# Eleven gate tiles moved out of the first attention into the delta net's levels, with the scan products of both directions on one bank

## The reference

```
mod = silu(c) @ w_ada + b_ada           # shift, scale, gate for both norms
h  = rmsnorm(x, norm_mix) * (1 + sc1) + sh1          # likewise hc from ctx
p  = h @ w_in                            # q,k,v | conv q,k,v | z | a,b | gates
qkv_d = silu(short_conv(qkv_d, conv_w)); q_d, k_d = l2norm(...)
g_attn, g_dn = split(sigmoid(gates + b_gate))
o_attn = windowed_attention(q, k, v, k_ctx, v_ctx, sink)
o_dn = gated_delta(q_d, k_d, v_d) forwards + backwards, context chunks first
     # per chunk: t_inv = inverse of unit lower triangular (A + I)
     # W = t_inv @ (k*beta*exp(G)); U = t_inv @ (v*beta)
     # v_new = U - W S;  o = q S + attn v_new;  S = S*g + k_tail v_new
x += gt1 * ((g_attn * (o_attn @ w_br_attn) + g_dn * (o_dn @ w_br_dn)) @ w_out)
```

## Time and profile before

| what | value |
|---|---|
| median of 3 runs | 1781.78 us (1777.49 to 1782.66) |
| profiled execution | 1772.43 us, its span 1770.6 us |
| PE busy | 1700.2 us, 96% |
| DVE, ACT, POOL busy | 1308.8, 1057.5, 161.3 us |
| bytes moved | 283.31 MB, mean 160 GB/s |
| projection's matmuls (L497) | 44.9 us to 256.4 us of the span |
| levels | about 261.5 us to 379.4 us of the span |

### The profile page before, as it was taken

How to read it: one execution, slowest core, us unless ns; L and a number is a source line. 1 busy time by engine, 2 the same in 40 slices (tenths; PEclk the granted TensorE clock), 3 DMA queues, 4 the chain that set the end, 5 groups by cost and what they waited for, 6 DMA issues and landing times.

```text
span 1770.6 us, 34144 instructions
## 1 busy us (share of the span) xinstructions
PE 1700.2 (96%) x11488; PEld 1513.5 (85%) x11488; DVE 1308.8 (74%) x2648; ACT 1057.5 (60%) x2182; POOL 161.3 (9%) x136
## 2 busy tenths in 40 slices
PE   7999997899999999999999999999899999999998
PEld 1877776689999978888899999999799899999997
DVE  3787677767989799667766666666776768878887
ACT  2545454445665699666555555555557666666666
POOL 0000003411548200000000000000010000010000
PEclk9999999999999999999999999999999999999999
DMA  8534441215455511455555555555364544555553
GB/s 303 186 99 140 156 154 60 84 47 199 161 178 178 166 37 48 166 191 196 193 185 185 189 189 184 186 188 189 119 209 142 176 141 133 177 184 185 187 181 129
DMA packets 77272, 283.31 MB, mean 160 GB/s; under 512 B 8576, under 2 KB 8576, under 8 KB 76928
## 3 DMA queue, kind: packets, MB, share of 16 engines
q1 hardware_dynamic: 77184, 282.16, 47.6%
HBM read 281.08 MB, written 1.05 MB: 159 GB/s over the span
## 4 chain that ended last, share of the span: by engine, by line
PE 80%; DVE 12%; ACT 4%; issue 2%; POOL 1%; DMA 1%; PEld 0%; PEldq 0%; ACTq 0%; POOLq 0%; DVEq 0%; SPq 0%
PE banks L921 20%; PE banks L909 17%; PE banks L1000 10%; PE banks L497 8%; PE banks L1156 7%; PE banks L1180 3%; PE banks L851 2%; DVE split L2444 2%; DVE arena L2440 2%; PE banks L465 1%; PE banks L1014 1%; PE banks L1116 1%; PE banks L821 1%; PE banks L541 1%; POOL split L2967 1%
## 5 line engine op out<-in xcount | busy, mean ns | idle before, releaser
L1529 ACT ACTIVATE split<-arena 128x512 fp32r<-128x512 f32 x492 | 308.9, 629 | 134.9 <-PE banks L909 76.8
L909 PEld LDWEIGHTS banks<-split 128*128 128x128 f32 x2880 | 355.4, 192 | 10.5 <-DVE split L2370 3.1
L921 PE MATMUL banks<-split 128*128 128x512 f32 x1536 | 361.9, 390 | 1.0 <-issue 1.0
L909 PE MATMUL banks<-split 128*128 128x256 f32 x2880 | 358.7, 283 | 3.2 <-DVE split L2370 2.3
L2462 DVE TENSOR_TENSOR split<-arena,split 128x512 fp32r<-128x512 f32 x396 | 270.6, 690 | 105.3 <-ACT split L1529 99.5
L921 PEld LDWEIGHTS banks<-split 128*128 128x128 f32 x1536 | 283.8, 188 | 57.3 <-issue 1.4
L1507 ACT ACTIVATE split<-arena 128x512 fp32r<-128x512 f32 x312 | 194.5, 627 | 112.3 <-PE banks L1156 52.9
L1000 PE MATMUL banks<-split 128*128 128x256 f32 x1728 | 216.8, 287 | 4.3 <-DVE split L2540 3.9
L1000 PEld LDWEIGHTS banks<-split 128*128 128x128 f32 x1728 | 211.9, 194 | 7.2 <-issue 6.0
L2517 DVE TENSOR_TENSOR split<-arena,split 128x512 fp32r<-128x512 f32 x180 | 123.7, 698 | 65.6 <-ACT split L1507 64.1
L497 PEld LDWEIGHTS banks<-split 128*128 128x128 f32 (+1 forms) x936 | 134.0, 194 | 28.5 <-issue 13.8
(11 more groups left out here) (421 smaller groups left out, 2311.5 us busy)
## 6 DMA issues: line engine op xcount, KB each, us to landing
arena<-wstream SPq DMA_DIRECT2D x525, 512.0 KB, 3.3
arena<-x_t SPq DMA_DIRECT2D x1, 2048.0 KB, 12.2
arena<-matsa SPq DMA_DIRECT2D x1, 1234.0 KB, 6.3
out_t<-arena SPq DMA_DIRECT2D x4, 256.0 KB, 2.0
arena<-mats SPq DMA_DIRECT2D x1, 576.0 KB, 8.1
arena<-crow SPq DMA_DIRECT2D x1, 512.0 KB, 7.1
arena<-rows SPq DMA_DIRECT2D x1, 512.0 KB, 3.9
arena<-mats SPq DMA_DIRECT2D x1, 449.0 KB, 4.3
```

Of the source, the lines that this page charges most:

```text
L909: mm = pe.matmul(ps[:, 4 + b, 0:S], w_parts[:, c, (2 * m + half) % 4, P * k:P * k + P], h_parts[:, e, 4 * half + k, :], start=(half == 0 a ...
L921: mm = pe.matmul(ps[:, 2 * tt + half, :], g_parts[:, e, j % 2, P * tt:P * tt + P], w_parts[:, c, (2 * m + half) % 4, :], start=(first and ...
L1529: act.activation(w_parts[:, 0, (2 * m + half) % 4, :], ring[:, peer_slot(m), 512 * half:512 * half + 512], ACT.Copy).then_inc(sem["w_hi"], 1)
```

## The change

1. The order of the stream is a list, `ORDER`. Behind tile t it puts the tails of `TAILS_BEHIND[t]`: one for POOL behind each of t = 10 to 17, three for DVE behind each of 25 to 28, and the other twelve between tiles 29 and 38. SP frees a tail's slot on `tail_sum` (POOL's) or `tail_done` (DVE's).
2. Twelve tails are now a multiplication on POOL and a sum on ACT (`sum_tail`): eight in `in_out(10)` to `in_out(17)`, one in level 3 of each block. DVE has twelve in the attention (three a group) and eight in the levels. `crow` is loaded and its SiLU taken early.
3. The attention keeps tiles 23, 24 and 25 (one in each of groups 0 to 2) and 26 (behind group 3); tile 27 stands where 38 stood.
4. Tiles 28 to 38 go into the levels as quarters of six matmuls on bank 7 (`fill_quarter`): one ahead of the level updates (`fill_before`) and one behind them (`fill_behind`). ACT rounds and moves out (`fill_hi`, `fill_out`), DVE subtracts one half in each level (`in_lo`).
5. Scan products of both directions share bank 6, one direction a level; `apply_inverse` writes banks 2d + 1 and 2d, so that the next block's products wait for `wu_ready` in place of `w_moved`. `z_turned` is folded into `y_done`. Half of the gates' sigmoid moves behind the levels.

```diff
+TAILS_BEHIND = {**{t: [("pool", t - 10)] for t in range(10, 18)}, **{t: [("dve", 3 * (t - 25) + q) for q in range(3)] for t in range(25, 29)}, ...
+ORDER = [x for t in range(39) for x in [("in", t)] + TAILS_BEHIND.get(t, [])]
             def load_freed_by_splits(lo, hi):
                 for n in range(lo, hi):
+                    kind, q = ORDER[n - RING - N_WIN]
+                    if kind == "in":
+                        sp.wait_ge(sem["in_lo"], 2 * q + 2)
+                    elif kind == "pool":
+                        sp.wait_ge(sem["tail_sum"], q + 1)
                     else:
+                        sp.wait_ge(sem["tail_done"], q + 1)
                     sp.dma_start(tile_at(n), wstream[n]).then_inc(loaded[n % RING], 16)
+            def fill_quarter(t, q):
+                if q == 0:
+                    pe.wait_ge(sem["proj_free"], 4 + t)
+                    ...
+                if q % 2 == 0:
+                    pe.wait_ge(sem["in_lo"], 2 * t + q // 2 + 1)
+                for k in (2 * q, 2 * q + 1):
+                    for c, e in PASSES:
+                        mm = pe.matmul(ps[:, 7, 0:S], ...)
+            def fill_before(step):
+                j, q = (step // 2, 1) if step % 2 else (step // 2 - 1, 3)
+                if 0 <= j < N_FILL:
+                    fill_quarter(FIRST_FILL + j, q)
+            def fill_behind(step):
+                if step // 2 < N_FILL:
+                    fill_quarter(FIRST_FILL + step // 2, 2 * (step % 2))
...
                     for d in range(2):
                         level_products(n, l, d)
+                    step = 6 * n + l - 1
...
+                    if n == 1 and l < 3:
+                        state_write(0, l - 1)
+                    if n >= 2 and l < 3:
+                        state_read(n - 1, l - 1)
+                    if n >= 2 and 3 <= l < 5:
+                        state_write(n - 1, l - 3)
+                    if n == 3 and l >= 5:
+                        out_write(2, l - 5)
...
+                    fill_before(step)
                     for d in range(2):
                         level_update(n, l, d)
...
+                    fill_behind(step)
 ACT, in in_out(t):
                 if 8 <= t < 20:
                     conv_silu(t - 8)
+                if 10 <= t < 18:
+                    sum_tail(t - 10)
+            def sum_tail(q):
+                tile = tile_at(AT["pool", q])
+                act.wait_ge(sem["tail_mult"], q + 1)
+                act.activation(tile, tile, ACT.Copy, accum_out=modT[:, ...]).then_inc(sem["tail_sum"], 1)
 ACT, in each level:
+                    if step % 2 == 0 and 0 < step <= 2 * N_FILL:
+                        fill_out(FIRST_FILL + step // 2 - 1)
+                    if 2 <= step < 2 * N_FILL - 2:
+                        fill_hi(step + 2)
...
+                    if l == 3:
+                        sum_tail(8 + n)
                     for d in range(2):
                         if n < 3 and l == 3:
                             decays(n + 1, d)
 DVE, in group g of the attention:
+                if g < 3:
+                    both_lo(25 + g)
+                for q in range(3):
+                    mod_tail(3 * g + q)
 DVE, in each level:
+                    i = 6 * n + l
+                    if 4 <= i < 2 * N_FILL:
+                        in_lo(FIRST_FILL + i // 2, i % 2)
+                    if l in (4, 6):
+                        mod_tail(12 + 2 * n + l // 6)
 POOL:
+            def mod_tail(q):
+                n = AT["pool", q]
+                pool.wait_ge(loaded[n % RING], 16 * (n // RING + 1))
+                pool.tensor_tensor(tile_at(n), tile_at(n), crow, ALU.mult).then_inc(sem["tail_mult"], 1)
+            pool.wait_ge(sem["conv_used"], 1)
+            for q in range(8):
+                mod_tail(q)
```

More of the change, by code:

```diff
@@ L1391, in _ @@
             tok_move(1)
-            in_out(38)
+            in_out(27)
             tok_move(2)
@@ L2179, in _ @@
             link(dve.tensor_copy(masks[:, :, 0:P], blocks))
-            tails = iter(range(EARLY_TAILS, 32))
-            for q in range(2):
-                mod_tail(next(tails))
+            both_lo(28)
             link(dve.tensor_tensor(gain3[:, 0, :], col("final_norm"), col("final_norm"), ALU.mult))
```

277 lines of the change are left out of this document (141 added, 136 removed).

## The result

Median of four executions 1814.63 us (1811.33 to 1817.49) against 1781.43 before: ratio 1.019, 95% interval 1.0164 to 1.0215. The forecast was 1800 with a range from 1776 to 1814: the sign was right, the size too small (18.5 us forecast, 33.2 measured). The profiled execution took 1816.22 us (span 1814.6), the one before 1772.43 (span 1770.6). These two are 43.8 us apart, the medians 33.2, since the profiled one of before was 9 us faster than its median. The stages are compared in the two traces; why other executions of before are slower is not seen in them.

What follows compares the result with a forecast made beforehand. PE was taken to bound the kernel (busy 96% of the span), with waits for DVE in the levels. Terms 19 - 2 - 24 + 0 + 25 + 0.5 = +18.5 us, put on the median 1781.8: 1800 us, range 1776 to 1814.

Steps and rivals of the forecast that it cites:

- The ring loop: Convolutions: each ACT step from tile 11 waits for a whole DMA, 8.0 us a tile against 5.49; +19 us.
- up to 0.9 us a tile: Convolutions: extra DVE time from POOL's multiplications beside its taps, hidden in the 8.0 us period, otherwise costing 3 us.
- Up to the first group: Ahead of the attention's first group: two tails leave from in front of DVE's logits(1), for which PE waits; -2 us.
- The attention: From the first group to the phase end: PE loses 34.3 us of work, less new waits and slow clock; -24 us.
- (c): Attention: PE's idle times bring slow-clock stretches as in tile 23; 3 us allowed.
- (a): Attention, group 1: the fourth product of scores(2) waits for DVE's logits(2); PE waits 3.8 us.
- (b): Attention, group 3: ACT's exponentials, logarithm and table loads delay first transposes 1.6 us and first weigh 3.8 us.
- Prologue: Prologue: two tails leave (2.4 us), both_lo(28) and both_lo(29) come (2.4); 0 us.
- The levels: Levels: quarters come on top where PE is full and fill only some idle time; +25 us, bounds 6 and 34.
- R1: Rival, convolutions: the ring's loop does not bind, they cost 0 to 3 us; total 1782; chance 0.15.
- R2: Rival, levels: quarters fit into PE's waits for DVE, costing 6 us in place of 25; down to 1772; chance 0.14.
- R3: Rival: idle times in convolutions and attention bring long slow clock, ten times, 15 us; 1815; chance 0.14 with another rival.

Runs made afterwards that it cites:

- e1: Changed kernel with ACT summing each POOL tail of the convolutions one tile earlier: ratio 1.0155 to the kernel before, tile 20 at 151.6.
- e4: e1 with POOL's eight convolution multiplications done on 8 of 1024 columns: span 1793.7, tile 20 at 139.8; no ratio taken.
- e6: Changed kernel with ACT's logarithm in group 1, DVE's squares behind logits(2), group 2's tails behind its output scaling: ratio 1.0137 to the kernel before, attention 67.0 us.
- e8: e6 with tile 26 in group 3 and tile 27 from the prologue behind it: ratio 1.014 to the kernel before.
- e12: e8 plus level 3's decays first and all tails on DVE, placed where it was seen idle: ratio 0.9975 to the kernel before, median 1773.95 us.
- e10_no_quarters: Changed kernel without the quarters' matmuls, ACT's and DVE's work for them kept: levels 141.7 us against 149.4; no ratio taken.
- e3_one_of_six: Changed kernel with one matmul of six in each quarter, ACT's and DVE's work kept: levels 144.85 us against 149.4; no ratio taken.

## Why the prediction was wrong, point by point

- **The ring loop (+19): right in mechanism.** Period 8.0 to 8.4 for a forecast 8.0, and e1 shows that it bound; from tile 13 to tile 19 the roundings fell behind by 15.1 us, as forecast. The term was +23.1, because POOL's price was wrong: "up to 0.9 us a tile" was read from a DVE tail that met only part of a POOL instruction. A whole meeting costs 2.0 to 2.2 us. Two meetings came ahead of the loop (1.8 and 2.1 us, from 87 to 92), where nothing hides them, and that is the 4 us. Without the loop POOL costs 11.8 us (e1 against e4), four times the 3 that I gave. The 10.5 us for DVE's work behind tile 19's rounding is a slip, its terms add up to 9.0; the rows say 10.9 before and 10.2 after.
- **Up to the first group (-2): -0.9.** Right in kind; behind late ropes and 4.2 us of idle PE tile 20 starts at half clock.
- **The attention (-24): the step that failed, (c), "I take 3 us".** The waits (a) and (b) came where I had them, 3.8 and 5.4 forecast for 3.1 and 3.3 us of idle time. But from 225 to the phase end, and 5 us beyond it, PE ran at half speed. My sum had PE busy for 54.6 + 3 - 1.5 = 56.1 us; it was busy for 70.6. The term was sized by the number of idle times, each with a loss as in the earlier trace rows. e6 shows that the clock falls without idle time in a group 3 that holds only small products, and e8 that one full tile in it keeps the clock up. The change took the full tiles out of group 3, which I had read only for waits. In the changed kernel the idle times of 1.0 and 2.25 us stand there too, so the fall has two possible triggers; taking them and the third away (e6) gave 10.7 us and left 24.7 us at half clock. In e12 the attention takes 59.7 us.
- **Prologue (0): +2.1**, its first 5 us at half clock (about 2.7 us lost by the estimate above).
- **The levels (+25, measured +31.6): the rows were priced nearly right, the clock was not.** I had the slow clock taken away and "PE clock at 1.00 in them". It was 0.86, 1.00, 0.96 and 1.00; 7.0 us lost to it before became 6.7. Where it fell can be read from update to update, in us, forecast and then measured:

| levels | 1 to 2 | 2 to 3 | 3 to 4 | 4 to 5 | 5 to 6 |
|---|---|---|---|---|---|
| block 0 | 4.6, 7.0 | 5.6, 5.4 | 4.9, 5.0 | 3.5, 5.4 | 4.2, 4.0 |
| block 1 | 5.1, 4.9 | 6.5, 6.5 | 7.0, 6.8 | 4.8, 5.3 | 4.2, 4.2 |
| block 2 | 5.1, 4.9 | 6.9, 7.2 | 7.0, 6.8 | 5.2, 6.3 | 4.2, 5.6 |
| block 3 | 6.1, 5.9 | 4.0, 4.7 | 4.0, 4.4 | 6.1, 5.9 | 3.5, 3.5 |

Most stand within 0.5 us, level 3 with its chain of ACT among them. The three largest misses are stretches at a low clock, 1 to 2 and 4 to 5 of block 0 and 5 to 6 of block 2:

```profile
275.30:282.40 7.10, 7.07 (x46) 6.01 (x46) 2.13 (x5) 1.62 (x5) 2.60 (x2) 0.60 0.24 76
293.00:298.20 5.20, 5.17 (x38) 4.27 (x34) 4.31 (x8) 1.67 (x5) 5.12 (x4) 0.67 0.00 2
376.50:382.20 5.70, 5.67 (x41) 4.81 (x42) 2.81 (x8) 4.37 (x11) 1.86 (x2) 0.70 0.38 129
```

By (1 - granted clock) times the length they lost 2.8, 1.7 and 1.7 us, 6.2 of the 6.6 missing: an estimate. What brings the clock down there no run shows.

- **R1 and R2 did not come.** R3 gave the nearest time (1815), for half of its reason: the clock fell for long in the attention, not in the convolutions, where it was 1.00 with PE idle for 23% of the time. That its ten losses of 1.5 us meet the measured time is luck.
- On medians the miss is 14.6 us, on the profiled executions 25.3 (43.8 against 18.5): 11.1 in the attention, 6.6 in the levels, 4.1 in the convolutions, 2.1 in the prologue, 1.1 up to the first group, 0.6 behind the levels, within the rounding. That the medians miss by less is luck too: the profiled execution of before was a quick one, and I put its distance on the forecast.

## What to carry to other kernels

When full tiles are taken out of a stage, look at what is left of the matmuls there, not only at the waits: a stretch of small products can cost up to twice its time with PE never idle. A forecast that prices every row and takes the full clock is short by what the clock takes: here 3 us allowed in the attention, none in the levels. Work moved from DVE to POOL and ACT is no relief while DVE is busy: price it at nearly the whole POOL instruction on DVE's account. In a ring loaded in order, a slot whose release is the last act of one step and whose content is the first need of the next puts a whole transfer into each step; one step of slack takes it out.

## What the runs showed of the hardware

- A POOL multiplication of 128x1024 (2.3 to 3.0 us) lengthens the DVE instruction that meets it by 2.0 to 2.2 us (e1), also one with a single tensor as its input (0.48 to 2.63, and 0.35 to 2.49 us in the changed kernel).
- The granted clock fell from 2.4 to 1.2 GHz behind 42 us in which PE was never idle for more than 0.28 us, and stayed there for 24.7 us at 97% busy (e6); and again behind 55.2 us without any idle time (e12). In the convolutions it stayed at 1.00 with PE idle by 18.6 of 80.3 us.
- Taking the quarters' matmuls out of the levels (34 us of work by the earlier trace rows) shortened them by 7.7 us (e10_no_quarters); the granted clock in blocks 0 to 2 went from 0.86, 1.00 and 0.96 to 0.75, 0.82 and 0.79.
- A single matmul of 128x256 among small ones takes 0.30 us of PE's time (e3_one_of_six, at full clock); in a row of 24 it is 0.13.
